# The best expert pairs of a head are sought among 64 sums of sorted key scores in place of 256

## The chip, the cores and the metric

The kernel runs on one core of one Trainium2 chip, as one program. The metric is the device time of one execution in microseconds. Three timed executions of the kernel before are known.

## What is computed

The kernel is one inference step of a trunk of two layers for 544 tokens: 512 of a prompt and 32 of a running stream. Each layer is a mixer (a linear recurrence beside an RWKV-7 state update), then PEER, a retrieval of single-neuron experts, then a small per-layer embedding. The change touches PEER alone. Cut to what matters:

```python
def peer_ffn(xn, wq, keys, u, v):        # per block of 128 tokens
    q = (xb @ wq).reshape(128, 8, 2, 128)                 # 8 heads, 2 query halves each
    s = jnp.einsum('thsc,hskc->thsk', q, keys)            # 128 key scores for each half
    top_s, top_i = lax.top_k(s, 16)                       # sorted, for each half
    cand = top_s[:, :, 0, :, None] + top_s[:, :, 1, None, :]      # 16 x 16 sums
    best_s, best_c = lax.top_k(cand.reshape(128, 8, 256), 16)
    i1 = take_along_axis(top_i[:, :, 0], best_c // 16)
    i2 = take_along_axis(top_i[:, :, 1], best_c % 16)
    e = i1 * 128 + i2                                     # 128 experts for each token
    gate = softmax(best_s)
    hid = einsum('td,tkd->tk', xb, u[e])
    return einsum('tk,tkd->td', gate * gelu(hid), v[e])
```

Both lists of 16 are sorted, falling. So the sum of entry a of the first list and entry b of the second (counted from 0) can be among the 16 best only if (a + 1)(b + 1) is at most 16. That holds for 50 of the 256 pairs.

## The kernel before, in words

**Dense experts.** For 384 of the tokens (three blocks of 128, tile `xh`/`xl`) the kernel computes the inputs of all 16384 experts, in 128 tiles of 128 experts: the PE loop `hidden` (L917 and L920) makes 24 matmuls of 128x384 for each tile (8 parts of the model width, three products of split numbers each). The weights of a tile come by two DMAs of 256 KB from SP (`load_u`), ACT makes the high parts (`high_u`, L1255), the vector engine DVE the low parts (`low_u`, L1887, twice for each tile), PE multiplies, ACT applies gelu (`gelu`, L1262) and stores the result (`save`, L1267, 192 KB). `uh` and `ul` have two buffers each, so ACT may split tile m only when PE has used tile m - 2, and DVE follows ACT.

**Gathered experts.** The other 160 tokens (128 of the prompt, and the 32 of the stream four times, with a quarter of the heads each) take their experts' rows by indirect DMAs from POOL (L620, 512 KB each); DVE takes the dot product of each row (`weigh_row`, L1898).

**Routing.** Which experts a token takes is decided on DVE by `route(part, order, ...)`, in ten parts, once for each block of 128 tokens. For order 1 (the gathered prompt tokens) and orders 3 to 5 (the dense blocks 0 to 2) a block has 16 score lists of 128 keys for 8 heads, for order 2 (the stream) 4 lists for 2 heads. Parts 0 to 4 find the 16 best keys of each list with MAX8 (L1814, L1825), FIND_INDEX8 (L1818, L1829) and MATCH_REPLACE8 (L1819). Part 5 forms all 256 sums of a head (L1834) and takes the first eight maxima (L1838). Part 6 finds their places and strikes them out (L1842, L1843). Part 7 takes the next eight maxima and their places (L1847, L1850). Part 8 subtracts the largest sum (L1855, and releases ACT's exponential), cuts each place into row and column by a shift and a mask (L1856, L1857, L1859) and calls `chosen(0)`, part 9 calls `chosen(1)` and forms gates and expert numbers. `chosen` picks key numbers by comparing each place with 16 numbers, multiplying and summing (L1800, L1803, L1805, 2048 elements each).

**Order of the work.** It is written out by hand. The stage goes over 64 pairs of tiles. Pairs 0 to 4 hold two parts of order 1 each, one behind each tile's `low_u`. Pairs 5 to 7 hold order 2: parts 0 to 3, 4 to 6, 7 to 9. Then there are three dense blocks, each with 10 pairs that hold one part of routing (orders 3 to 5), two `low_u` of two instructions each, and two rows, and 8 pairs that build the gate matrix of the block (`hot`, L1909, and the gate matmuls L954), with four or five rows. At the end stand two pairs with nothing else. During the first 8 pairs of dense blocks 1 and 2, ACT also stores an eighth of the gate matrix of the block before each time (`save_gates`, L1307, 1 MB each, in pieces of 512 bytes); these stores and those of L1267 share ACT's DMA queue, and `gelu` waits until the store of tile m - 2 has landed. After this stage comes one over the 128 tiles of output weights (L993).

**Memory.** All tiles lie at fixed addresses, handed out one behind the other; the table of constants `cn` is among the first, and nearly everything behind it starts where it ends.

Of the kernel before, what the change touches and what calls it, by code (L numbers as in the profile page):

```python
# [9 lines left out]
U32 = mybir.dt.uint32  # L10
# [53 lines left out]
CN = {}  # L64
_at = 0
for _name, _n in [("ident", P), ("ones", P), ("heads", P), ("iota", P), ("causal", P), ("eye", C),
                  ("level", LEVELS * C), ("reset", MW), ("fold", DEC)]:
    CN[_name] = _at
    _at += _n
NCN = _at  # L70

SO = {"conv": (0, 12), "lru": (24, 4), "shift": (32, 14)}
NSO = 60
# [50 lines left out]
def constants():  # L124
    c = np.zeros((P, NCN), np.float32)
    i = np.arange(P)
    c[:, CN["ident"]:CN["ident"] + P] = np.eye(P)
    c[:, CN["ones"]:CN["ones"] + P] = 1.0
    c[:, CN["heads"]:CN["heads"] + P] = (i[:, None] // HD == i[None] // HD)
    c[:, CN["iota"]:CN["iota"] + P] = i[None]  # L130
    s, t = i[:, None] % C, np.arange(C)[None]
    c[:, CN["eye"]:CN["eye"] + C] = s == t
    c[:, CN["causal"]:CN["causal"] + C] = s < t
    c[:, CN["causal"] + C:CN["causal"] + P] = s <= t
    for k in range(LEVELS):
        b = 1 << k
        off = (s // (2 * b) == t // (2 * b)) & (s // b % 2 == 0) & (t // b % 2 == 1)
        c[:, CN["level"] + k * C:CN["level"] + (k + 1) * C] = off
    r = np.ones(MW)
    r[[k * C for k in range(NCH)] + [DEC0]] = 0.0  # L140
    c[:, CN["reset"]:CN["reset"] + MW] = r[None]
    c[:, CN["fold"]:CN["fold"] + DEC] = i[:, None] % DEC == np.arange(DEC)[None]
    return c

# [11 lines left out]
def trunk(nc, x, p, small, const, spread, mixw, wkv0, w_in, w_out, wq, keys, ut, u, v, wple, y, small_out, wkv_out):  # L156
    ctx = ExitStack()
    with ctx:
# [1241 lines left out]
        def _(dve):  # L1400
# [24 lines left out]
            for L in range(DEPTH):  # L1425
# [356 lines left out]

                def route(part, order, n, src, keep):
                    heads = n // 2
                    cand = s2[:, 0:heads * 256].rearrange("p (q a b) -> p q a b", q=heads, a=TOPK)
                    shape = [P, heads, TOPK, TOPK]
                    picks = heads * TOPK
                    eq = s2[:, 0:heads * 256].rearrange("p (q k j) -> p q k j", q=heads, k=TOPK)
# [3 lines left out]
                        return s2[:, q * NK:(q + 1) * NK]  # L1792

                    def pair_of(q):
                        return s2[:, q * 256:(q + 1) * 256]

                    def chosen(w):
                        b3 = bf[:, w, 0:heads, :].rearrange("p q k -> p (q k)").unsqueeze(2).to_broadcast([P, picks, TOPK])
                        i3 = iota[:, 0:TOPK].unsqueeze(1).to_broadcast([P, picks, TOPK])
                        tt(eq3, b3, i3, ALU.is_equal)  # L1800
                        dve.drain()
                        tfs = tf[:, 0:n].rearrange("p (q w) k -> p q w k", w=2)
                        tt(eq, eq, tfs[:, :, w, :].unsqueeze(2).to_broadcast(shape), ALU.mult)  # L1803
                        dve.drain()
                        nc.vector.tensor_reduce(sel_t[:, 1 + w, 0:picks], eq3, AX.X, ALU.add)  # L1805
                        dve.drain()
# [20 lines left out]
                    elif part == 4:  # L1827
                        for q in range(n):
                            mi(ti[:, q, 8:16].bitcast(U32), tv[:, q, 8:16], key(q))  # L1829
                        dve.drain()  # L1830
                    elif part == 5:
                        copy(tf[:, 0:n], ti[:, 0:n].bitcast(U32))
                        tvs = tv[:, 0:n].rearrange("p (q w) k -> p q w k", w=2)
                        tt(cand, tvs[:, :, 0, :].unsqueeze(3).to_broadcast(shape),  # L1834
                           tvs[:, :, 1, :].unsqueeze(2).to_broadcast(shape), ALU.add)
                        dve.drain()
                        for q in range(heads):
                            mx(bv[:, q, 0:8], pair_of(q))  # L1838
                        dve.drain()
                    elif part == 6:  # L1840
                        for q in range(heads):
                            mi(bi[:, q, 0:8].bitcast(U32), bv[:, q, 0:8], pair_of(q))  # L1842
                            mr(pair_of(q), bv[:, q, 0:8], pair_of(q), NEG)  # L1843
                        dve.drain()
                    elif part == 7:
                        for q in range(heads):
                            mx(bv[:, q, 8:16], pair_of(q))  # L1847
                        dve.drain()
                        for q in range(heads):
                            mi(bi[:, q, 8:16].bitcast(U32), bv[:, q, 8:16], pair_of(q))  # L1850
                        dve.drain()
                    elif part == 8:
                        copy(gsum[:, 0:heads], bv[:, 0:heads, 0:1])
                        dve.drain()
                        tt(bv[:, 0:heads], bv[:, 0:heads], gsum[:, 0:heads].unsqueeze(2).to_broadcast([P, heads, TOPK]), ALU.subtract).then_inc(best_ready, 1)  # L1855
                        ts(ba[:, 0, 0:heads].bitcast(U32), bi[:, 0:heads].bitcast(U32), 4, None, ALU.logical_shift_right)  # L1856
                        ts(ba[:, 1, 0:heads].bitcast(U32), bi[:, 0:heads].bitcast(U32), 15, None, ALU.bitwise_and)  # L1857
                        dve.drain()
                        copy(bf[:, :, 0:heads], ba[:, :, 0:heads].bitcast(U32))  # L1859
                        dve.drain()  # L1860
                        chosen(0)
                    else:
                        chosen(1)
                        dve.wait_ge(gexp, L * 5 + order)
                        nc.vector.tensor_reduce(gsum[:, 0:heads], bv[:, 0:heads], AX.X, ALU.add)
                        dve.drain()
                        dve.reciprocal(gsum[:, 0:heads], gsum[:, 0:heads])
                        dve.drain()
                        gate = sel_t[:, 0, :] if keep is None else keep[0]
                        last = tt(gate.rearrange("p (q k) -> p q k", q=heads), bv[:, 0:heads],  # L1870
                                  gsum[:, 0:heads].unsqueeze(2).to_broadcast([P, heads, TOPK]), ALU.mult)
                        if keep is not None:
                            ts(sel_t[:, 1, 0:picks], sel_t[:, 1, 0:picks], float(NK), float(L * NK * NK), ALU.mult, ALU.add)
                            dve.drain()
                            tt(sel_t[:, 1, 0:picks], sel_t[:, 1, 0:picks], sel_t[:, 2, 0:picks], ALU.add)
                            dve.drain()
                            copy(keep[1].bitcast(U32), sel_t[:, 1, 0:picks]).then_inc(rows_ready, 1)
                            dve.drain()
                            dve.sem_inc(routed, 1)
                        else:  # L1880
                            last.then_inc(routed, 1)
# [212 lines left out]
```

## Time and profile before

| | |
|---|---|
| three timed executions | 4023.65, 4023.8, 4024.65 us; median 4023.8 |
| the profiled execution's own time | 4028.22 us |
| its span | 4026.4 us |
| mean granted clock of TensorE, of full speed | 0.959 |
| busy share of the span | PE 90%, DVE 74%, ACT 41%, POOL 23% |
| DMA over the span | 890.04 MB, 221 GB/s |
| instructions | 65006, of them 6048 on DVE |

The page names instructions by engine and line. A line of the page's fifth part gives the busy time of a group of alike instructions, the mean of one, and then the time for which the engine sat idle just before them and what released it. The expert stage of the first layer lies between 608 and 1374 us of the span, that of the second between 2604 and 3371 us.

### The profile page before, as it was taken

To read this page: it belongs to the slowest core of one execution; us is meant where nothing else is said; L and a number is where in the kernel's file an instruction comes from. 1 tells how busy PE (TensorE), PEld (TensorE's weight loads), DVE (VectorE), ACT (ScalarE), POOL (GpSimd) and SP (SyncE) were. 2 spreads that over 40 slices of the span, in tenths; PEclk is the share of its full clock that TensorE was granted. 3 is DMA by queue.
4 is the path that set the end of the run, shared out by engine and by line. 5 is a ranking of instruction groups with operands and counts; after the bars stand their busy time and mean duration, and the time that the engine had idled before them with its cause. 6 is when DMAs were issued, how large, how long until landed. Compare 5 with 4: busy or idle time off the path is not lost.

```text
span 4026.4 us, 65006 instructions
## 1 busy us (share of the span) xinstructions
PE 3629.5 (90%) x24642; PEld 3255.2 (81%) x24642; DVE 2970.4 (74%) x6048; ACT 1654.1 (41%) x3067; POOL 923.9 (23%) x742
## 2 busy tenths in 40 slices
PE   8878897898999799999898878988989897999998
PEld 8867697898988688888787767978989896888877
DVE  5765228989899588888367653199998995888872
ACT  4322123394848433333233221233939393333331
POOL 3200040222223233333031000302323232333320
PEclk9989998999999899999998989999999998999999
DMA  3100135689797999998221001357898989999971
GB/s 118 57 2 3 43 93 182 237 268 344 259 328 270 324 389 381 379 379 312 77 79 47 2 5 53 118 173 246 277 327 275 334 268 340 386 379 380 378 269 62
DMA packets 544661, 890.04 MB, mean 221 GB/s; under 512 B 37824, under 2 KB 361952, under 8 KB 543584
## 3 DMA queue, kind: packets, MB, share of 16 engines
q1 hardware_dynamic: 311872, 444.84, 31.4%
q0 software_dynamic: 92416, 336.17, 23.9%
q10 hardware_dynamic: 140064, 104.88, 8.0%
q8 instruction: 197, 3.23, 0.3%
q14 instruction: 112, 0.92, 0.1%
HBM read 778.07 MB, written 107.67 MB: 220 GB/s over the span
## 4 chain that ended last, share of the span: by engine, by line
PE 67%; DVE 19%; ACT 4%; DMA 3%; issue 3%; ACTq 2%; DVEq 1%; SPq 0%
PE ps L993 26%; PE ps L659 10%; PE ps L643 7%; PE ps L917 6%; PE ps L920 3%; PE ps L954 3%; DVE m L1887 3%; DMA expert_inputs<-m 3%; DVE m L1898 2%; ACT m L1289 2%; PE ps L778 1%; PE ps L786 1%; ACTq L1307 1%; PE ps L635 1%; DVE m L1677 1%
## 5 line engine op out<-in xcount | busy, mean ns | idle before, releaser
L993 PE MATMUL ps<-m,m 128*128 128x512 f32 x4608 | 1066.3, 393 | 12.9 <-DVE m L1959 12.9
L993 PEld LDWEIGHTS ps<-m,m 128*128 128x128 f32 x4608 | 866.8, 188 | 212.2 <-issue 13.5
L917 PE MATMUL ps<-m,m 128*128 128x384 f32 x4096 | 841.7, 348 | 45.3 <-ACT m L1262 45.3
L917 PEld LDWEIGHTS ps<-m,m 128*128 128x128 f32 x4096 | 735.0, 195 | 49.1 <-ACT m L1262 48.6
L620 POOL DMA_INDIRECT m<-in_u,m x320 | 354.0, 1106 | 1092.7 <-DVE m L1898 897.9
L920 PE MATMUL ps<-m,m 128*128 128x384 f32 x2048 | 462.4, 348 | 123.8 <-DVE m L1887 123.7
L620 POOL DMA_INDIRECT m<-in_v,m x320 | 359.7, 1124 | 785.8 <-DVE ps L1971 555.5
L1361 ACT ACTIVATE m<-m 128x1024 fp32r<-128x1024 f32 x256 | 271.5, 1061 | 653.2 <-PE ps L993 651.4
L920 PEld LDWEIGHTS ps<-m,m 128*128 128x128 f32 x2048 | 374.3, 195 | 143.1 <-DVE m L1887 143.0
L659 PE MATMUL ps<-m,m 128*128 128x272 f32 x3648 | 468.7, 290 | 5.4 <-ACT m L1059 4.6
L1255 ACT ACTIVATE m<-m 128x512 fp32r<-128x512 f32 x512 | 318.6, 624 | 374.8 <-PE ps L920 270.7
L659 PEld LDWEIGHTS ps<-m,m 128*128 128x128 f32 x3648 | 463.6, 189 | 8.7 <-issue 5.4
L1887 DVE TENSOR_TENSOR m<-m,m 128x512 fp32r<-128x512 f32 x512 | 331.8, 687 | 83.3 <-ACT m L1255 81.0
L592 POOL TENSOR_TENSOR m<-m,m 128x1024 fp32r<-128x1024 f32 x76 | 191.0, 2515 | 628.1 <-ACT m L1059 628.1
L1971 DVE SCALAR_TENSOR_TENSOR ps<-m,m,ps 128x1024 f32<-128x1024 f32 x254 | 326.0, 1284 | 4.6
L1944 DVE TENSOR_TENSOR m<-m,m 128x1024 fp32r<-128x1024 f32 x256 | 312.0, 1219 | 14.3 <-ACT m L1361 14.3
L1898 DVE CUSTOM_DVE_ANT_0 m<-m,ps 128x1024 f32<-128x1024 f32 x256 | 306.3, 1217 | 6.5 <-issue 0.5
L643 PE MATMUL ps<-m,m 128*128 128x272 f32 x1152 | 274.5, 400 | 39.3 <-DVE m L1756 20.6
L643 PEld LDWEIGHTS ps<-m,m 128*128 128x128 f32 x1152 | 223.3, 194 | 87.4 <-DVE m L1756 21.5
L1909 DVE TENSOR_SCALAR m<-m,m 128x128 f32<-128x128 f32 x768 | 213.0, 347 | 70.5 <-PE ps L954 55.3
L1289 ACT ACTIVATE m<-m,m 128x128 f32<-128x128 f32 x768 | 243.9, 392 | 0.5
L1262 ACT ACTIVATE m<-ps 128x384 f32<-128x384 f32 x256 | 123.8, 484 | 259.1 <-PE ps L920 183.7
(265 smaller groups left out, 3964.7 us busy)
## 6 DMA issues: line engine op xcount, KB each, us to landing
m<-in_ut SPq DMA_DIRECT2D x512, 256.0 KB, 5.3
m<-in_v SPq DMA_DIRECT2D x256, 512.0 KB, 6.2
expert_inputs<-m ACTq DMA_DIRECT2D x256, 192.0 KB, 3.8
gate_matrix<-m ACTq DMA_DIRECT2D x48, 1024.0 KB, 10.2
m<-gate_matrix SPq DMA_DIRECT2D x256, 192.0 KB, 5.2
m<-expert_inputs SPq DMA_DIRECT2D x256, 192.0 KB, 6.8
m<-in_w_in SPq DMA_DIRECT2D x44, 512.0 KB, 3.8
m<-in_wq SPq DMA_DIRECT2D x32, 512.0 KB, 3.8
```

Source lines behind the costliest of these rows:

```text
L620: pool.indirect_dma_start(ug[r % NUG], None, table[:, :], bass.IndirectOffsetOnAxis(ap=index.bitcast(U32), axis=0)).then_inc(row_in[r % NU ...
L643: last = mm(ps[:, bank + a, 0:HALF], wslot[:, slot, k, :], rhs[:, n, a * HALF:(a + 1) * HALF], start=(n == 0), stop=(n == len(ks) - 1))
L659: last = mm(ps[:, 2 * j + a, 0:HALF], lhs[j][:, k, :], rhs[:, k, a * HALF:(a + 1) * HALF], start=(k + w == 0), stop=(k == KD - 1 and w == 2))
L917: mm(ps[:, j, 0:DT], uh[j][:, k, :], x_[:, k, :], start=(k == 0 and x_ is xh), stop=False)
L920: last = mm(ps[:, j, 0:DT], ul[j][:, k, :], xh[:, k, :], start=False, stop=(k == KD - 1))
L993: last = mm(ps[:, 2 * t + a, :], lhs[s][:, t * BLK:(t + 1) * BLK], rhs[s][:, a * 512:(a + 1) * 512], start=(n + w == 0), stop=(n == NK - 1 ...
L1255: av(uh[m % 2][:, ks, :], uraw[m % NU][:, ks, :], ACT.Copy).then_inc(uh_ready, 1)
L1289: av(oneA[:, g % 2, j, :], iota, ACT.Abs, bias=sel[:, 1, t:t + 1])
L1887: tt(ul[m % 2][:, ks, :], uraw[m % NU][:, ks, :], uh[m % 2][:, ks, :].bitcast(F32), ALU.subtract).then_inc(ul_ready, 1)
L1898: nc.vector.tensor_tensor_reduce(row, row, other, 1.0, 0.0, ALU.mult, ALU.add, at).then_inc(row_used, 1)
L1944: tt(vl[n % NV], vraw[n % NV], vh[n % NV].bitcast(F32), ALU.subtract).then_inc(vl_ready, 1)
L1971: last = stt(acc, row, w, acc, ALU.mult, ALU.add)
```

## The change

The 256 sums become 64, in four pieces: row 0 with 16 columns, rows 1 to 3 with 8, rows 4 to 7 with 4, rows 8 to 15 with 1. These hold the 50 pairs. The searches of parts 5 to 7 (L1838, L1842, L1843, L1847, L1850) go over 64 elements for each head. A place in the shorter list is no longer 16 times row plus column: `STARTS` holds the place at which each row begins, in 16 new columns of the constant table. The key number of the row is found in `chosen(0)` as the sum, over all rows that begin at or before the place, of the difference between that row's key number and the one before it. The column is the place masked with 15, 7, 3 or 0, and the mask is worked out by three comparisons with 16, 40 and 56. Part 5 has four additions in place of one, part 8 eight instructions more, so DVE has 11 instructions more for each of the ten orders of the program. Everything else keeps its place in the order. The constant table grows from 1700 to 1716 columns, and the tiles laid out behind it start 64 bytes later.

```diff
+CANDS = [(0, 1, 16), (1, 3, 8), (4, 4, 4), (8, 8, 1)]
+STARTS = [0, 16, 24, 32, 40, 44, 48, 52, *range(56, 64)]
+NCAND = 64
...
-                    cand = s2[:, 0:heads * 256].rearrange("p (q a b) -> p q a b", q=heads, a=TOPK)
+                    cand = s2[:, 0:heads * NCAND].rearrange("p (q c) -> p q c", q=heads)
...
-                        return s2[:, q * 256:(q + 1) * 256]
+                        return s2[:, q * NCAND:(q + 1) * NCAND]
...
-                        i3 = iota[:, 0:TOPK].unsqueeze(1).to_broadcast([P, picks, TOPK])
-                        tt(eq3, b3, i3, ALU.is_equal)
-                        dve.drain()
-                        tfs = tf[:, 0:n].rearrange("p (q w) k -> p q w k", w=2)
-                        tt(eq, eq, tfs[:, :, w, :].unsqueeze(2).to_broadcast(shape), ALU.mult)
+                        i3 = (iota[:, 0:TOPK] if w else const_of("starts", TOPK)).unsqueeze(1).to_broadcast([P, picks, TOPK])
+                        tt(eq3, b3, i3, ALU.is_equal if w else ALU.is_ge)
+                        dve.drain()
+                        tfs = tf[:, 0:n].rearrange("p (q w) k -> p q w k", w=2)[:, :, 1, :] if w else ba[:, 0, 0:heads]
+                        tt(eq, eq, tfs.unsqueeze(2).to_broadcast(shape), ALU.mult)
...
-                        tt(cand, tvs[:, :, 0, :].unsqueeze(3).to_broadcast(shape),
-                           tvs[:, :, 1, :].unsqueeze(2).to_broadcast(shape), ALU.add)
+                        at = 0
+                        for i0, rows_, cols_ in CANDS:
+                            tt(cand[:, :, at:at + rows_ * cols_].rearrange("p q (a b) -> p q a b", a=rows_),
+                               tvs[:, :, 0, i0:i0 + rows_].unsqueeze(3).to_broadcast([P, heads, rows_, cols_]),
+                               tvs[:, :, 1, 0:cols_].unsqueeze(2).to_broadcast([P, heads, rows_, cols_]), ALU.add)
+                            at += rows_ * cols_
...
-                        ts(ba[:, 0, 0:heads].bitcast(U32), bi[:, 0:heads].bitcast(U32), 4, None, ALU.logical_shift_right)
-                        ts(ba[:, 1, 0:heads].bitcast(U32), bi[:, 0:heads].bitcast(U32), 15, None, ALU.bitwise_and)
-                        dve.drain()
-                        copy(bf[:, :, 0:heads], ba[:, :, 0:heads].bitcast(U32))
+                        pos, low = bf[:, 0, 0:heads], ba[:, 1, 0:heads]
+                        firsts = tf[:, 0:n].rearrange("p (q w) k -> p q w k", w=2)[:, :, 0, :]
+                        copy(pos, bi[:, 0:heads].bitcast(U32))
+                        copy(ba[:, 0, 0:heads, 0:1], firsts[:, :, 0:1])
+                        tt(ba[:, 0, 0:heads, 1:TOPK], firsts[:, :, 1:TOPK], firsts[:, :, 0:TOPK - 1], ALU.subtract)
+                        dve.drain()
+                        ts(low, pos, 16.0, -8.0, ALU.is_ge, ALU.mult)
+                        ts(bf[:, 1, 0:heads], pos, 40.0, -4.0, ALU.is_ge, ALU.mult)
+                        dve.drain()
+                        stt(low, low, 15.0, bf[:, 1, 0:heads], ALU.add, ALU.add)
+                        dve.drain()
+                        ts(bf[:, 1, 0:heads], pos, 56.0, -3.0, ALU.is_ge, ALU.mult)
+                        dve.drain()
+                        tt(low, low, bf[:, 1, 0:heads], ALU.add)
+                        dve.drain()
+                        copy(bf[:, 1, 0:heads].bitcast(U32), low)
+                        dve.drain()
+                        tt(low.bitcast(U32), bf[:, 1, 0:heads].bitcast(U32), bi[:, 0:heads].bitcast(U32), ALU.bitwise_and)
+                        dve.drain()
+                        copy(bf[:, 1, 0:heads], low.bitcast(U32))
                         dve.drain()
                         chosen(0)
```

## Rows read from the trace of the kernel before

**Rows 1.** The page, part five: PE's second group of the dense experts.
```profile
L920 PE MATMUL ps<-m,m 128*128 128x384 f32 x2048 | 462.4, 348 | 123.8 <-DVE m L1887 123.7
```

**Rows 2.** Windows: length, each engine's busy us (xinstructions), PE clock, DMA share, GB/s.
```profile
635.00:692.10 57.10, 41.39 (x194) 39.45 (x193) 54.45 (x168) 16.03 (x27) 5.21 (x5) 0.85 0.38 130
723.10:758.70 35.60, 34.20 (x194) 33.16 (x193) 34.78 (x144) 13.18 (x25) 9.16 (x8) 1.00 0.83 281
758.70:791.20 32.50, 28.31 (x146) 27.67 (x145) 31.94 (x92) 9.84 (x18) 6.87 (x6) 0.89 0.67 231
791.20:816.70 25.50, 19.90 (x98) 19.23 (x97) 24.57 (x29) 9.34 (x15) 4.52 (x4) 0.87 0.56 194
928.30:966.00 37.70, 34.83 (x196) 33.63 (x196) 32.76 (x129) 12.71 (x24) 9.16 (x8) 1.00 1.07 368
966.00:998.60 32.60, 26.94 (x144) 25.98 (x143) 32.11 (x92) 9.80 (x20) 6.87 (x6) 0.95 1.06 357
998.60:1026.00 27.40, 20.23 (x99) 19.55 (x98) 24.77 (x30) 9.37 (x16) 4.59 (x5) 0.88 0.73 244
...
3134.50:3171.40 36.90, 34.38 (x195) 33.42 (x194) 32.71 (x129) 12.63 (x24) 9.16 (x8) 1.00 1.06 359
...
1500.00:1900.00 400.00, 400.00 (x1736) 325.43 (x1735) 354.53 (x410) 141.50 (x193) 134.04 (x119) 1.00 1.00 375
```

**Rows 3.** DVE's timeline, parts 5 to 8 of dense block 1, first layer: start, length.
```profile
966.17 0.29 DVE L1832 CAST m<-m 128x256 f32<-128x256 uint32 x1
966.38 2.29 DVE L1834 TENSOR_TENSOR m<-m 128x2048 f32<-128x2048 f32 x1
968.73 2.72 DVE L1838 MAX8 m<-m 128x8 f32<-128x256 f32 x8
971.57 1.22 DVE L1898 CUSTOM_DVE_ANT_0 m<-m,ps 128x1024 f32<-128x1024 f32 x1
...
976.26 0.09 DVE L1842 MATCH_VALUE_LOAD m<-m,m 128x8 f32 x1
...
982.77 1.22 DVE L1898 CUSTOM_DVE_ANT_0 m<-m,ps 128x1024 f32<-128x1024 f32 x1
...
987.47 2.70 DVE L1847 MAX8 m<-m 128x8 f32<-128x256 f32 x8
...
993.62 1.22 DVE L1898 CUSTOM_DVE_ANT_0 m<-m,ps 128x1024 f32<-128x1024 f32 x1
...
998.32 0.29 DVE L1853 COPY m<-m 128x8 f32<-128x8 f32 x1
998.68 0.29 DVE L1855 TENSOR_TENSOR m<-m,m 128x128 f32<-128x128 f32 x1
998.89 0.22 DVE L1856 TENSOR_SCALAR m<-m 128x128 uint32<-128x128 uint32 x1
...
999.69 2.29 DVE L1800 TENSOR_TENSOR m<-m,m 128x2048 f32<-128x2048 f32 x1
```

**Rows 4.** DVE's timeline: the same searches over 128 elements, dense block 2.
```profile
1135.40 0.08 DVE L1818 MATCH_VALUE_LOAD m<-m,m 128x8 f32 x1
...
1135.92 0.08 DVE L1818 MATCH_VALUE_LOAD m<-m,m 128x8 f32 x1
...
1155.06 3.18 DVE L1825 MAX8 m<-m 128x8 f32<-128x128 f32 x16
```

**Rows 5.** DVE's timeline: small instructions of which each needs the one before.
```profile
680.86 0.22 DVE L1873 TENSOR_SCALAR m<-m 128x128 f32<-128x128 f32 x1
681.16 0.29 DVE L1875 TENSOR_TENSOR m<-m 128x128 f32<-128x128 f32 x1
681.52 0.23 DVE L1877 CAST m<-m 128x128 uint32<-128x128 f32 x1
```

**Rows 6.** ACT's timeline, gelu of every tile: an undisturbed pair of tiles.
```profile
928.31 0.49 ACT L1262 ACTIVATE m<-ps 128x384 f32<-128x384 f32 x1 [1.39 <-PE ps L920]
...
936.63 0.49 ACT L1262 ACTIVATE m<-ps 128x384 f32<-128x384 f32 x1 [0.86 <-PE ps L920]
```

**Rows 7.** Waits from 930 to 1000 us: total, times, longest.
```profile
ACT m L1262 <- DMA expert_inputs<-m: 16.1, 4, 6.0
```

**Rows 8.** DMA queues from 928 to 975 us: ACT's queue, packets, MB, share.
```profile
q10 hardware_dynamic: 11073, 6.85, 45.9%
```

More of the change, by code:

```diff
@@ L66 @@
 for _name, _n in [("ident", P), ("ones", P), ("heads", P), ("iota", P), ("causal", P), ("eye", C),
-                  ("level", LEVELS * C), ("reset", MW), ("fold", DEC)]:
+                  ("level", LEVELS * C), ("reset", MW), ("fold", DEC), ("starts", TOPK)]:
     CN[_name] = _at
@@ L141, in constants @@
     c[:, CN["reset"]:CN["reset"] + MW] = r[None]
+    c[:, CN["starts"]:CN["starts"] + TOPK] = np.array(STARTS)[None]
     c[:, CN["fold"]:CN["fold"] + DEC] = i[:, None] % DEC == np.arange(DEC)[None]
```

## The prediction

> **What bounds the kernel now.** The change touches only routing on DVE, so I first asked where DVE sets the pace. The page's fifth part gives the answer for the dense experts: PE idled 123.8 us before its last product, nearly all for `low_u` on DVE [rows 1]. The window view says in which pairs. One undisturbed pair of tiles takes 8.32 us from gelu to gelu, which is PE alone [rows 6]. In parts 1 to 4 of dense block 0 a pair takes 35.60 / 4 = 8.9 us. In parts 5 to 7 it takes 32.50 / 3 = 10.8 us, with DVE busy for 31.94 and PE for 28.31. Parts 8 and 9 take 25.50, of which DVE works 24.57 [rows 2]. There DVE is the bound, and the searches over 256 sums are exactly its parts 5 to 7. The same holds for order 1 (635.0 to 692.1: DVE 54.45 of 57.10, PE 41.39) [rows 2].
>
> Dense blocks 1 and 2 differ. Parts 1 to 4 need no more DVE time than in block 0, yet take 37.70 us (36.90 in the fastest of four such windows), with a DMA share of 1.06 or 1.07 [rows 2], and ACT's gelu waits for its stores to land, 16.1 us in 70 [rows 7]. ACT's queue, where the gate matrix goes out in 512-byte pieces, takes 45.9% of the DMA engines' time [rows 8]. In parts 5 to 7 (32.60 us) the DMA share is still 1.06 [rows 2], so DVE and the DMA engines are both full. This second bound is what the sum must respect.
>
> **DVE time of one order with 8 heads.**
> Part 5 now runs from 966.17 to 971.57, 5.40 us [rows 3]. Eight MAX8 over 256 take 2.72 us, one every 0.33 us; sixteen over 128 take 3.18 us, one every 0.19 [rows 3, 4]. That is 1.06 ns for each element, so one over 64 should come every 0.126 us: 1.6 us less. The sums shrink from 2048 elements to 512, 1.6 us less at 1.04 ns each, with three more instructions at some 0.07 (estimate): 1.4 less. Part 5 saves 3.0 and lasts 2.4.
> Part 6 runs from 976.26 to 982.77, 0.80 us a head after its closing gap [rows 3]. A head's two searches over 128 take 0.52 [rows 4], so over 64 they take 0.38. It saves 3.3 and lasts 3.2.
> Part 7 (987.47 to 993.62, 6.15 us [rows 3]) saves 1.6 on MAX8 and half of part 6's on FIND_INDEX8, 1.7. It saves 3.3 and lasts 2.9.
> Part 8 grows. Its small work takes 1.37 us now (998.32 to 999.69) [rows 3]. The new chain is 13 instructions, mostly each needing the last. Such a step costs 0.30 us behind a scalar instruction and 0.36 behind others [rows 5], one that needs nothing 0.1 to 0.2 (0.21 at 998.68 [rows 3]). I get 0.36 + 0.21 + 0.2 + 0.36 + 0.43 + 0.36 + 0.30 + 4 x 0.36 = 3.7 us, so 2.3 more. ACT's exponential is released before this chain and is no later. `chosen` does the same three instructions of 2048 elements.
> Together: 9.6 less, 2.3 more, 7.3 us of DVE time less.
>
> **What of it reaches the end.**
> *Dense block 0, twice (one in each layer).* Parts 5 to 7 would need 32.5 - 9.6 = 22.9 us of DVE, but PE needs 3 x 8.4 = 25.2. So these pairs save 7.3, and DVE gains up to 2.3 us on PE. It can use this lead in part 8, as far as the two buffers let it run ahead; I take 1.7 of the 2.3. Parts 8 and 9 get 0.6 longer. Sum: 2 x -6.7 = -13.4 (bounds -5.5 and -7.2 each).
> *Dense blocks 1 and 2, four times.* Here the DMA pace is late next. Parts 1 to 4 ran at it: 36.9 to 38.0 us for four pairs, 9.35 on the mean of my four windows (two of them stand in [rows 2]). At that pace three pairs take 28.1 us, a saving of 4.5 (from 32.6), and 3.9 with the 0.6. Sum: 4 x -3.9 = -15.6. The bounds are the PE floor, -7.2 each, and -1.5 each, if the queue of stores, which the slow pairs let run down, now grows instead.
> *Order 1, twice.* No rows and no gate stores are moved there (DMA share 0.38 [rows 2]). Three tiles need 3 x 1.2 + 2.4 + 3.2 + 2.9 = 12.1 of DVE against 12.5 of PE, so nearly all 7.3 show: 2 x -7.1 = -14.2 (bounds -6 and -7.4).
> *Order 2, twice, with 2 heads.* At these rates its searches save 2 us and part 8's chain of short instructions adds about 1.7, but the saving falls mostly into the pair of parts 4 to 6, where PE is the bound, and the addition into the pair of parts 7 to 9, where DVE is: 2 x +0.5 = +1.0 (bounds -0.5 and +1 each).
> *At nothing:* 64 bytes more of constants for each partition at the start, behind 2 MB of inputs; the first gather starts 7 us earlier, but its rows are due at fixed pairs; the second half of each block (`hot`) and the output stage are PE's.
>
> Sum: -13.4 - 15.6 - 14.2 + 1.0 = -42.2 us. The profiled execution took 4028.2, so its like should take 3986.0. The median of the timed runs is 4.4 below the profiled one, so I predict 3981.6.
>
> **One rule that speaks against the change.** All tiles behind the constants move by 64 bytes. The gate matrix before its stores lies at byte 16512 + 4 x 36680, which is 160 past a multiple of 256, and will lie at 224 past. No row here shows the price of an offset; the stores already start off such a boundary and take 45.9% of the DMA time [rows 8]. I take nothing for it in the sum.
> The Trainium skill, DMA: Bandwidth & Descriptors, section "How a descriptor splits into AXI transactions", says that a read that does not start at a multiple of 256 bytes is fetched from the multiple below, and the unused bytes cost as well. By it a piece of 512 bytes would fetch 736 bytes in place of 672, some 10% more. No run so far shows whether that matters.
>
> **The rivals.**
> *B, the DMA keeps up.* If pairs at PE's pace are possible in blocks 1 and 2, each of the four gives -6.8 in place of -3.9: 3970.0. For it speaks that the pairs moved 357 GB/s in parts 5 to 7 and 368 in parts 1 to 4, so there is some room; against it the share of 1.06 in both [rows 2]. Chance 0.12.
> *C, the DMA gives less than before.* If the pieces of ACT's queue take 10% longer, its 45.9% [rows 8] make the saturated pairs 4.6% slower: 9.35 to 9.78 us, for 7 pairs in each of four blocks, +12: 3993.6. A queue that never drains would look alike. Chance 0.13. (The rule above is one way to this.)
> *D, short searches don't get shorter.* Below 128 elements the fixed part may rule. If 64 elements cost what 128 cost, 40 searches give back 0.07 us each, 2.7 us of DVE for an order: all of it in order 1 (+5.4), the lead and 0.4 in block 0 (+4.2), nothing where DMA is the bound: 3991.2. For it: nothing shorter than 128 is in the trace. Against it: the step from 256 to 128 is as large as the elements explain [rows 3, 4]. Chance 0.11.
> *E, slower.* The moved addresses cost where the DMA engines are full for long: in the output stage, DMA share 1.00, 375 GB/s, PE busy 400 of 400 us [rows 2]. That stage has 4608 matmuls, 1736 in 400 us, so 1062 us. From 4.0% on (42.2 / 1062) it eats the gain; at 6% it gives +64, 4045.6. Against it: nothing changes there but 64 bytes of offset. Chance 0.02.
> That the change doesn't do what it says I rule out: 110 more instructions stand in DVE's program, 11 for each of ten orders, as they should.
> TensorE's clock was at 1.2 GHz for a while in the DVE-bound windows (mean 0.89, 0.87, 0.95, 0.88, against 1.00 in the others) [rows 2], each time where PE had been waiting. While DVE is the bound such a dip is free. With PE busy it should not come in parts 5 to 7; if it came, it would cost up to 3.6 us in a window (11% of 32.5). That is inside the range.
>
> **How the numbers follow.** Forecast 0.60, B 0.12, C 0.13, D 0.11, E 0.02, and 0.02 for a gain lost in ways I don't see. A difference under 0.2% (8 us) is about what a measurement of this kernel can't tell from no change. With all the good bounds at once the gain is 59 (3965), with all the bad ones 26 (3998); these ends hold B, C and D. Faster 0.96, same 0.02, slower 0.02.
>
> **What would show it.** MAX8 at L1838's place every 0.13 us, and part 6 near 3.2 us. Parts 5 to 7 of block 0 in about 25 us, with PE full and its clock at 1.00; in blocks 1 and 2 in about 28, with more waits of gelu for its stores. Part 8's small work 3.7 us. Parts 8 and 9 nearly as long as before. If blocks 1 and 2 save as much as block 0, B is right; if their parts 1 to 4 get longer too, C; if the searches show 0.19, D. The output stage must stay at 4.15 us a tile.

## The result, and the profile after

| | median of the timed executions | lowest to highest |
|---|---|---|
| before, 4 executions | 4023.73 us | 4023.33 to 4024.65 |
| changed kernel, 4 executions | 3993.24 us | 3987.98 to 3995.32 |

The ratio is 0.9916, with a 95% interval of 0.9903 to 0.9928. So the change saves 30.5 us of the 42.2 forecast. A second comparison (e2 below) gave 0.9909 (0.9894 to 0.9924), 36.9 us. The profiled execution has a span of 3989.4 us against 4026.4, 37.0 less. So a single execution or a single comparison moves by several us here, which is part of what follows. One execution of the kernel before, beside e5 to e8, took 5509.13 us at a granted clock of 0.608 and is left out of every comparison below.

The page of the changed kernel answers to [rows 1] with its line L925. The chain of waits that ended last stands above it.

```profile
PE 68%; DVE 16%; DMA 5%; ACT 5%; issue 3%; ACTq 2%; DVEq 1%; SPq 0%
...
L925 PE MATMUL ps<-m,m 128*128 128x384 f32 x2048 | 457.8, 346 | 90.3 <-DVE m L1912 90.0
```

PE's wait for `low_u` fell from 123.8 to 90.3 us. In the chain, the transfers rose from 3% to 5% and DVE fell from 19% to 16%.

**The searches themselves.** Parts 5 to 8 on DVE's timeline in dense block 0 (start, length), which answer to [rows 3]:

```profile
748.42 0.41 DVE L1837 CAST m<-m 128x256 f32<-128x256 uint32 x1
748.75 0.88 DVE L1841 TENSOR_TENSOR m<-m 128x128 f32<-128x128 f32 x4
749.70 1.11 DVE L1847 MAX8 m<-m 128x8 f32<-128x64 f32 x8
750.93 1.22 DVE L1923 CUSTOM_DVE_ANT_0 m<-m,ps 128x1024 f32<-128x1024 f32 x1
...
755.63 0.09 DVE L1851 MATCH_VALUE_LOAD m<-m,m 128x8 f32 x1
...
758.95 1.22 DVE L1923 CUSTOM_DVE_ANT_0 m<-m,ps 128x1024 f32<-128x1024 f32 x1
...
763.64 1.11 DVE L1856 MAX8 m<-m 128x8 f32<-128x64 f32 x8
...
766.60 1.22 DVE L1923 CUSTOM_DVE_ANT_0 m<-m,ps 128x1024 f32<-128x1024 f32 x1
...
771.30 0.29 DVE L1862 COPY m<-m 128x8 f32<-128x8 f32 x1
...
774.88 2.29 DVE L1805 TENSOR_TENSOR m<-m,m 128x2048 f32<-128x2048 f32 x1
```

Part 5 takes 2.51 us (748.42 to 750.93), forecast 2.4. Part 6 takes 3.32 (755.63 to 758.95), forecast 3.2. Part 7 takes 2.96 (763.64 to 766.60), forecast 2.9. Part 8's small work takes 3.58 (771.30 to 774.88), forecast 3.7. Together DVE saves 18.06 - 8.79 = 9.3 us and pays 2.2, so 7.1 for an order; the forecast was 7.3.

**Where it reached the end.** Windows of the changed kernel, with the columns of [rows 2]. In order: order 1 (with the first pair of order 2); block 0 parts 1 to 4, 5 to 7, 8 and 9; block 1 the same three; block 2 the same three; the output stage.

```profile
632.40:682.70 50.30, 38.94 (x194) 37.98 (x193) 46.84 (x183) 16.07 (x28) 5.22 (x5) 0.83 0.44 147
713.50:748.70 35.20, 34.11 (x194) 33.15 (x193) 34.74 (x144) 13.14 (x25) 9.17 (x8) 1.00 0.83 281
748.70:773.70 25.00, 25.00 (x146) 25.00 (x145) 24.13 (x103) 9.92 (x19) 6.91 (x7) 1.00 0.96 319
773.70:801.20 27.50, 20.31 (x99) 19.58 (x98) 24.78 (x29) 9.32 (x16) 4.59 (x4) 0.88 0.53 190
912.70:950.60 37.90, 34.80 (x196) 33.62 (x196) 32.96 (x129) 12.75 (x24) 9.29 (x8) 1.00 1.07 368
950.60:981.50 30.90, 29.23 (x164) 27.96 (x163) 25.01 (x106) 9.44 (x19) 6.89 (x6) 1.00 1.07 390
981.50:1006.90 25.40, 15.96 (x79) 14.97 (x77) 24.41 (x27) 9.39 (x17) 4.59 (x4) 0.87 0.67 222
1118.40:1154.90 36.50, 34.27 (x193) 33.17 (x193) 33.00 (x130) 12.81 (x24) 9.15 (x8) 1.00 1.07 366
1154.90:1189.00 34.10, 27.80 (x146) 27.48 (x146) 24.43 (x104) 9.63 (x19) 7.02 (x7) 0.90 1.01 342
1189.00:1214.80 25.80, 19.31 (x98) 18.63 (x97) 24.66 (x29) 9.32 (x15) 4.58 (x4) 0.87 0.64 218
...
1500.00:1900.00 400.00, 399.76 (x1753) 325.59 (x1751) 346.98 (x400) 139.93 (x189) 127.92 (x113) 1.00 0.95 358
```

In block 0 parts 5 to 7 went from 32.50 to 25.00 us, with PE busy for all of it and its clock at 1.00. In block 1 they took 30.90 and in block 2 even 34.10, against 32.60 and 32.5 before, though DVE's work fell from about 32 to 25.01 and 24.43. The DMA share is over 1.00 there in both. The waits of the changed kernel from 950 to 982 us (total, times, longest) say what holds them:

```profile
ACT m L1267 <- DMA expert_inputs<-m: 12.9, 3, 5.1
...
ACT m L1260 <- issue: 3.0, 1, 3.0
...
ACT m L1260 <- DMA m<-in_ut: 2.7, 2, 1.4
```

That is gelu waiting for its own stores. Over the whole execution these waits came to 95.7 us in 24, against 75.0 in 20 before. In block 2 one of them lasted 8.19 us. It stands in ACT's timeline (start, length, engine; the idle time before it in brackets):

```profile
1163.79 4.07 ACTq L1272 DMA_DIRECT2D expert_inputs<-m  x1
1167.90 0.46 ACTq L1312 DMA_DIRECT2D gate_matrix<-m  x1
1168.47 0.64 ACT L1260 ACTIVATE m<-m 128x512 fp32r<-128x512 f32 x1 [4.19 <-issue]
1177.30 0.49 ACT L1267 ACTIVATE m<-ps 128x384 f32<-128x384 f32 x1 [8.19 <-DMA expert_inputs<-m]
```

Put together by the sections of the stage (each counted from the start of one gelu to that of a later one, order 1 from the first `low_u` of the stage; both layers added, one profile each):

| section | before | changed | difference | forecast |
|---|---|---|---|---|
| order 1, pairs 0 to 4 | 139.4 | 125.6 | -13.8 | -14.2 |
| order 2, pairs 5 to 7 | 69.5 | 68.6 | -0.9 | +1.0 |
| block 0, parts 1 to 9 | 187.0 | 175.2 | -11.8 | -13.4 |
| blocks 1 and 2, parts 1 to 9, four in all | 387.7 | 378.2 | -9.6 | -15.6 |
| everything else | | | -0.9 | 0 |
| span | 4026.4 | 3989.4 | -37.0 | -42.2 |

### The profile page after: what moved, and what is told of

The parts are those of the page before. It is cut to its first block, busy times and chain, and to the rows that moved or that the text cites. A ratio compares the mean times of both kernels' runs of the same rounds, so it can differ in the third digit from the quotient of the medians.

```text
span 3989.4 us, 65176 instructions
## 1 busy us (share of the span) xinstructions
PE 3621.7 (91%) x24642; PEld 3248.9 (81%) x24642; DVE 2908.6 (73%) x6158; ACT 1652.7 (41%) x3067; POOL 925.1 (23%) x742
## 3 DMA queue, kind: packets, MB, share of 16 engines
q1 hardware_dynamic: 311872, 444.85, 31.6%
q10 hardware_dynamic: 140064, 104.88, 8.1%
## 4 chain that ended last, share of the span: by engine, by line
PE 68%; DVE 16%; DMA 5%; ACT 5%; issue 3%; ACTq 2%; DVEq 1%; SPq 0%
PE ps L998 27%; PE ps L664 11%; PE ps L648 7%; PE ps L922 7%; DMA expert_inputs<-m 5%; PE ps L925 4%; PE ps L959 3%; DVE m L1912 2%; ACT m L1294 2%; DVE m L1923 2%; PE ps L783 1%; PE ps L791 1%; ACTq L1312 1%; PE ps L640 1%; DVE m L1682 1%
## 5 line engine op out<-in xcount | busy, mean ns | idle before, releaser
L998 PE MATMUL ps<-m,m 128*128 128x512 f32 x4608 | 1067.8, 394 | 11.5 <-DVE m L1984 11.5
L925 PE MATMUL ps<-m,m 128*128 128x384 f32 x2048 | 457.8, 346 | 90.3 <-DVE m L1912 90.0
L925 PEld LDWEIGHTS ps<-m,m 128*128 128x128 f32 x2048 | 373.3, 194 | 104.1 <-DVE m L1912 104.1
L648 PE MATMUL ps<-m,m 128*128 128x272 f32 x1152 | 275.1, 401 | 38.6 <-DVE m L1761 20.6
## 6 DMA issues: line engine op xcount, KB each, us to landing
gate_matrix<-m ACTq DMA_DIRECT2D x48, 1024.0 KB, 12.8
```

The source lines that it names most:

```text
L648: last = mm(ps[:, bank + a, 0:HALF], wslot[:, slot, k, :], rhs[:, n, a * HALF:(a + 1) * HALF], start=(n == 0), stop=(n == len(ks) - 1))
L925: last = mm(ps[:, j, 0:DT], ul[j][:, k, :], xh[:, k, :], start=False, stop=(k == KD - 1))
L998: last = mm(ps[:, 2 * t + a, :], lhs[s][:, t * BLK:(t + 1) * BLK], rhs[s][:, a * 512:(a + 1) * 512], start=(n + w == 0), stop=(n == NK - 1 ...
```

## The experiments

Two theories stood against each other for the missing part. DMA-BOUND: what DVE frees in blocks 1 and 2 goes to the DMA engines, which move the gate stores, the weights, the rows and the small stores there at their limit. ADDRESSES: the 64 bytes by which everything moved make the stores dearer.

**e1 to e4, one chip.** e1 and e3 add spare columns to the constants, to the kernel before and to the changed one:

```diff
-                  ("level", LEVELS * C), ("reset", MW), ("fold", DEC)]:
+                  ("level", LEVELS * C), ("reset", MW), ("fold", DEC), ("spare", 16)]:
...
-                  ("level", LEVELS * C), ("reset", MW), ("fold", DEC), ("starts", TOPK)]:
+                  ("level", LEVELS * C), ("reset", MW), ("fold", DEC), ("starts", TOPK), ("spare", 48)]:
```

> The kernel before with 16 spare columns behind its constants, so that all tiles behind them start 64 bytes later, as in the change, and nothing else differs. Theory DMA-BOUND (in blocks 1 and 2 the time freed on DVE goes to the DMA engines, whatever the addresses): within 2 us of the kernel before, parts 5 to 7 of those blocks 32.5 us as before. Theory ADDRESSES (the offset makes ACT's stores about 10% dearer): parts 1 to 4 of blocks 1 and 2 get longer than 37.4 us by 1 to 2 us each, the whole 4 to 12 us slower. The Trainium skill, DMA: Bandwidth & Descriptors, section How a descriptor splits into AXI transactions, would have the pieces at 224 bytes past a multiple of 256 fetch 736 bytes in place of 672.

> The changed kernel as it is, again. Both theories: 3988 to 3996 us. DMA-BOUND: the sections of block 0 and of order 1 are the same as in the first profile to 0.5 us, and the spread between executions lies in blocks 1 and 2, parts 1 to 9 (first profile: 94.1, 96.4, 93.5, 94.2 us). If the spread lies elsewhere, the theory is wrong about it.

> The changed kernel with 48 more spare columns, so that the tiles behind the constants lie 256 bytes later than before the change and at the same place within a multiple of 256 as then. DMA-BOUND: as e2, within 3 us. ADDRESSES: faster than e2 by 4 to 12 us, all of it in blocks 1 and 2.

Measured: e1 4029.59 us against 4026.69 for the kernel before, a ratio of 1.0005 (0.9996 to 1.0014). e2 3989.77 us, ratio 0.9909 (0.9894 to 0.9924). e3 3994.72 us, 0.9916 (0.9902 to 0.9929). Moving all tiles by 64 bytes costs nothing that shows, and moving them back to the old place within 256 bytes gains nothing. The interval leaves room for 0.14%, 5.6 us, and e1's median is 2.9 us up, a little more than the 2 expected of DMA-BOUND. But parts 1 to 4 of blocks 1 and 2, which ADDRESSES had to make 1 to 2 us longer each, add up to 150.2 us in e1 against 149.7, and the packets of ACT's queue took the same share of the DMA engines' time. Its line on the page of the kernel before, and on that of e1 (packets, MB, share):

```profile
q10 hardware_dynamic: 140064, 104.88, 8.0%
```
```profile
q10 hardware_dynamic: 140064, 104.88, 8.0%
```

ADDRESSES falls, and with it the part of rival C that rested on it.

The sections of e1 to e3 also answer the question of the spread. Parts 5 to 7 of block 0 are 25.0 us in every profile of the changed kernel. Parts 1 to 9 of blocks 1 and 2 add up to 387.7 us in the first profile of the kernel before and 380.6 in e1; to 378.2 in the first profile of the changed kernel, 373.6 in e2 and 376.4 in e3. So the same program differs there by 5 to 7 us from one execution to the next. e2 expected that the spread would lie there alone; it does not quite, since order 1 of e3's first layer took 66.5 us instead of 62.8, and of e1 72.4 instead of 69.6. That excess stands before the first gelu, where PE waited 3.11 and 2.18 us for nothing that the profile shows; from the first gelu on, the order took as long as in the first profiles.

e4 moves rows away from the pairs that the DMA engines bound:

```diff
-                n += 2 if b is None or i < ROUTE_PAIRS else 4
+                if b is None or i < ROUTE_PAIRS:
+                    n += 1 if b and 0 < i < 8 else 2
+                else:
+                    n += 5 if b < NB - 1 and i > ROUTE_PAIRS else 4
```

> The changed kernel with one gathered row in place of two in pairs 1 to 7 of dense blocks 1 and 2, and five in place of four in pairs 11 to 17 of blocks 0 and 1. This takes 0.5 MB of 3.5 from each DMA-bound pair. DMA-BOUND: parts 1 to 7 of blocks 1 and 2 fall from about 69 us to PE's floor of 58 to 60 each, 9 us each, four times; pairs 11 to 17 stay at 12.6 us if DVE (11.3 + 1.2 = 12.5 us) still fits; the whole 30 to 38 us faster than e2, near 3958. If DVE doesn't fit there, 28 pairs get 0.2 to 0.5 us longer and the gain is 20 to 30. ADDRESSES: the stores stay dear, but the bytes fall as well, so it gives a smaller gain of 10 to 20 us.

Measured: 3964.96 us, ratio 0.9845 (0.9832 to 0.9859), 24.8 us faster than e2 and less than the 30 to 38 expected. Windows of e4: four gate pairs of block 0, then parts 1 to 4, 5 to 7, 8 and 9 of block 2.

```profile
833.30:883.80 50.50, 50.33 (x333) 49.39 (x333) 49.91 (x124) 49.40 (x122) 19.20 (x20) 1.00 0.93 323
1116.10:1149.50 33.40, 33.40 (x195) 33.29 (x194) 29.75 (x130) 12.88 (x25) 4.57 (x4) 1.00 1.05 368
1149.50:1174.40 24.90, 24.90 (x145) 24.90 (x144) 20.12 (x94) 9.75 (x18) 3.24 (x4) 1.00 1.08 371
1174.40:1201.20 26.80, 19.12 (x99) 18.45 (x98) 25.47 (x31) 9.35 (x15) 4.55 (x4) 0.87 0.63 216
```

Parts 1 to 7 now run at PE's floor in block 2, with the DMA engines just able to follow (368 and 371 GB/s, at a share of 1.05 and 1.08, as high as where PE had to wait), and the gate pairs hold five rows with DVE busy for 49.91 of 50.50 us and no loss. In block 1 parts 1 to 4 still took 36.5 and 35.8. Another part of the expected gain was lost again in parts 8 and 9: 27.8, 26.8, 28.5 and 26.3 us in place of 25.4, 28.0, 26.5 and 24.2 in e2. The likely reason is that while gelu waits for the DMA, PE and DVE work ahead of it, and these windows are bounded by gelu; such work is done before part 8's window opens. The first profile shows it: 164 matmuls of PE in parts 5 to 7 of block 1 where block 0 has 146, and 79 in parts 8 and 9 where block 0 has 99. A stall of this kind is paid back in part, and only the sum over parts 1 to 9 can be read.

**e5 and e6, the stores out of the way.** In both kernels the gate matrix is stored only at the end of the stage, and ACT's waits for these stores move with it (left out here). What is stored is then the matrix of the last block three times, so the results are wrong and only the times of the sections are of use:

```diff
-                    if b is not None and b > 0 and i < 8:
-                        save_gates(b - 1, i)
-                    elif pair == PART - 1:
-                        for q in range(8):
-                            save_gates(NB - 1, q)
+                    if pair == PART - 1:
+                        for to in range(NB):
+                            for q in range(8):
+                                save_gates(to, q)
```

> The changed kernel in which the gate matrix of blocks 0 and 1 is not stored during blocks 1 and 2: the staging tile is stored three times at the end of the stage instead (so all blocks get the gates of the last, and the last pairs of the stage get longer by some 40 us). Read by sections only. DMA-BOUND: parts 5 to 7 of blocks 1 and 2 take 25.0 us as in block 0, parts 1 to 4 35 to 35.5 or less. If something else than the stores holds these pairs back, they stay at 28 us or more.

> The same edit on the kernel before. DMA-BOUND: parts 1 to 4 of blocks 1 and 2 fall from 37.4 to about 35.4 us, parts 5 to 7 stay at 32.3 to 32.5 (DVE is the bound there), so that e5 against e6 gives about 5.5 us for each of six dense blocks, 47 us with order 1. If the stores were no bound in parts 1 to 4, those stay at 37.

Measured, one execution each. Windows of e5, block 1, parts 1 to 4, 5 to 7, 8 and 9:

```profile
917.30:950.70 33.40, 33.40 (x194) 33.26 (x194) 32.94 (x130) 13.19 (x25) 9.15 (x8) 1.00 0.93 313
950.70:975.70 25.00, 25.00 (x146) 25.00 (x145) 24.05 (x102) 9.92 (x19) 6.89 (x7) 1.00 0.94 324
975.70:1003.30 27.60, 20.16 (x98) 19.43 (x97) 24.95 (x30) 9.34 (x16) 4.58 (x4) 0.88 0.53 189
```

Windows of e6, block 1, parts 1 to 4, 5 to 7:

```profile
928.90:962.20 33.30, 33.30 (x193) 33.16 (x192) 32.84 (x130) 13.13 (x24) 9.10 (x8) 1.00 0.95 318
962.20:994.50 32.30, 27.43 (x147) 26.47 (x146) 31.81 (x91) 9.88 (x18) 6.92 (x7) 0.95 0.69 234
```

Without the stores all four blocks behave like block 0, in parts 5 to 7 of both layers: 25.0 in e5, 32.2 to 32.5 in e6. Gelu waits for no store any more in either. Between the two kernels the spans differ by 4128.4 - 4072.4 = 56.0 us, and parts 1 to 9 of blocks 1 and 2 by 367.5 - 339.8 = 27.7 us. That is the 27 us that rival B gave these blocks (4 x 6.8). So the searches are worth 56 us where the DMA has room, the kernel gets 37 in its profile, and the stores of the gate matrix in the same pairs take nearly all of the difference. This settles that it is these stores; whether by their bytes or by their place in ACT's queue is left to e11. I had expected less: 5.5 us for each dense block and 47 in all, where block 0 gave 6.0, blocks 1 and 2 6.9 each, and the whole 56, and parts 1 to 4 at 35.4 us, where PE's floor was 33.4. The last two pairs got longer by some 60 us each layer and not by 40, in both kernels alike.

**e7, the price of the chain in part 8.** The short searches stay, the cutting of places is the old one:

```diff
-                        copy(pos, bi[:, 0:heads].bitcast(U32))
...
+                        ts(ba[:, 0, 0:heads].bitcast(U32), bi[:, 0:heads].bitcast(U32), 4, None, ALU.logical_shift_right)
+                        ts(ba[:, 1, 0:heads].bitcast(U32), bi[:, 0:heads].bitcast(U32), 15, None, ALU.bitwise_and)
+                        dve.drain()
+                        copy(bf[:, :, 0:heads], ba[:, :, 0:heads].bitcast(U32))
```

> The changed kernel with the kernel before's cutting of places (shift and mask, and the comparison with equal), so that the eight added instructions of part 8 are gone and the short searches stay; experts are then the wrong ones. Prediction's account: part 8's small work falls from 3.7 to 1.4 us, parts 8 and 9 get shorter by 2.3 us in each of six dense blocks and in order 1 twice, 1.7 in order 2 twice: up to 22 us faster than the changed kernel, if nothing else catches it. RIVAL: lead of DVE over PE hides the chain, less than 8 us.

Measured: 3970.21 us, ratio 0.9862 (0.9846 to 0.9878), 19.6 us faster than e2 by the medians and 18.9 by the two ratios. Parts 8 and 9 of block 0 fall from 27.5 to 25.6 and from 27.2 to 25.3 us, order 1 from 63.1 to 60.1 and from 62.7 to 60.3. In blocks 1 and 2 parts 1 to 9 went from 373.6 to 366.4 us together, 1.8 for each block. The rival, that DVE's lead hides the chain, falls. I had let the lead hide 1.7 of 2.3 us in each block. In truth 1.9 of 2.2 show. Why the lead hides so little was not tried. e7 picks other experts and so gathers other rows; that this costs or saves nothing is not shown.

**e8, the rows moved in the kernel before.** The edit of e4.

> The rows moved as in e4, on the kernel before. DMA-BOUND: parts 1 to 4 gain the DMA's 2 us and DVE's row, parts 5 to 7 are DVE's there and lose one row of 1.2 us each: 32.5 to 29; together 5 to 7 us for each of the four blocks, 20 to 28 us. Then e4 minus this is what the short searches give with room on the DMA side, 40 us or more. RIVAL (the gain of e4 comes from the rows alone): e8 gains as much as e4 did, and the searches add no more than the 37 us of e2.

Measured: 4000.70 us against 4026.3, ratio 0.9936 (0.9922 to 0.995), 25.6 us. Parts 5 to 7 of blocks 1 and 2 took 28.7, 28.7, 28.7 and 28.3 us, as expected. The moved rows gain about the same in either kernel (24.8 and 25.6), and the searches are worth 36.1 us with the rows moved (61.7 - 25.6) as against 36.9 without. These are the rival's numbers, and the first expectation (40 or more) missed. e8 alone would speak against DMA-BOUND; the sections say why it does not: moving rows frees not only the DMA engines but also 1.14 us of DVE in each of these pairs, and what the searches could still save there down to PE's 25.0 us is then only 3.6 in place of 7.3, and parts 8 and 9 of e4 give back 1.2 us of that in each block (109.4 us for the four against 104.6 in e8).

**e9 and e10, better versions.** e9 is e4 with no rows in pairs 8 and 9 of blocks 1 and 2 and five in the gate pairs of block 2; e10 takes them out of block 0 as well:

```diff
+                if b is None:
+                    n += 2
+                elif i < ROUTE_PAIRS:
+                    n += 0 if i > 7 else 1 if b and i > 0 else 2
+                else:
+                    n += 5
```

> As e4, and besides no rows at all in pairs 8 and 9 of dense blocks 1 and 2, where DVE is the bound (part 8 with its longer chain, part 9); these eight rows of a layer go to the last eight gate pairs, of block 2, five in place of four. Each row taken away there frees 1.14 us of DVE: parts 8 and 9 of those blocks fall from 27 to about 22.5 us, four times, the gate pairs of block 2 stay at 101 us. The whole 14 to 18 us faster than e4, near 3948. RIVAL: PE or the short lead takes over in parts 8 and 9 and less than 8 us show.

> As e9, and no rows in pairs 8 and 9 of block 0 either; of these four rows of a layer two go to the first gate pairs of blocks 0 and 1 (five rows each) and two to pair 62, where DVE is idle for 29 of 32 us. Parts 8 and 9 of block 0 fall from 27.5 to 23 us, twice; the first gate pairs, 14.8 us with DVE 13.1 busy, get up to 1 us longer each. The whole 5 to 9 us faster than e9. RIVAL: the two rows in pair 62 lengthen that pair, where the DMA engines are full, by 1 to 3 us each layer, and the gain is 2 to 5.

Measured: e9 3950.98 us, ratio 0.9813 (0.98 to 0.9827), 14.0 faster than e4 by the medians, 12.9 by the ratios, at the low end of the 14 to 18 expected. Parts 8 and 9 of blocks 1 and 2 took 23.9, 23.3, 24.1 and 22.7 us, most of them above the 22.5 expected. e10 3947.52 us, 0.9807 (0.9794 to 0.982), 3.5 faster than e9 by the medians, with intervals that overlap, so the 5 to 9 expected did not come and whether e10 is faster than e9 is open. In e10 parts 8 and 9 of block 0 went to 22.5 us (27.5 in e9's first layer). Pairs 62 and 63 together, of which pair 62 got two rows, went from 40.8 us in the first layer and 41.2 in the second to 42.6 and 42.5, which is the rival's price. Windows of e10, parts 8 and 9 of blocks 0 and 1:

```profile
773.20:795.70 22.50, 18.83 (x98) 18.15 (x98) 20.29 (x21) 9.35 (x15) 0.00 (x0) 0.92 0.46 157
968.50:992.10 23.60, 18.49 (x98) 17.81 (x97) 21.07 (x24) 9.31 (x15) 0.00 (x0) 0.93 0.61 207
```

e10 has the lowest median of this study: 78.7 us under the kernel before on its chip (4026.21).

**e11 and e12, queue or bytes.** Gelu waits for small stores that stand behind a big one in the same queue, so the order in the queue could be what costs, and not the bytes. Both versions store the gate matrix from SP's queue, one pair later, in the changed kernel and in e10:

```diff
+                    if b and 0 < i < 9 and m % 2 == 0:
+                        q = i - 1
+                        sp_.wait_ge(gmat_out, (L * NB + b) * GB)
+                        sp_.dma_start(gate_d[:, 16 * q:16 * q + 16, (b - 1) * BLK:b * BLK], stage[:, 16 * q:16 * q + 16, :]).then_inc(gate_saved[q // 2], 16)
...
-                    if b is not None and b > 0 and i < 8:
-                        save_gates(b - 1, i)
-                    elif pair == PART - 1:
+                    if pair == PART - 1:
```

> The changed kernel with the gate matrix of blocks 0 and 1 stored from SP's queue, one eighth at a time one pair later (pairs 1 to 8 of the next block), so that ACT's small stores no longer stand behind a store of 1 MB and ACT no longer issues into a full queue. The bytes are the same. BYTES (the DMA engines' throughput is the bound, about 350 to 375 GB/s): parts 1 to 9 of blocks 1 and 2 stay at 91 to 96 us each and the whole within 5 us of e2. QUEUE (gelu waits for its store behind the big one in the same queue, and that is what holds PE back): those parts fall to 88 us or less and the whole is 10 to 25 us faster than e2; gelu's waits for DMA go away.

> The same on the fastest version, e10, where the rows are moved as well. Parts 1 to 4 of block 1, 36 us there against PE's 33.4, are what is left of the DMA bound. BYTES: within 3 us of e10. QUEUE: parts 1 to 4 of block 1 fall to 33.5 and the whole is 3 to 6 us faster.

Measured: e11 3995.45 us, ratio 0.9922 (0.9908 to 0.9936), 5.7 slower than e2 by the medians. e12 3960.51 us, 0.9829 (0.9814 to 0.9844), 13.0 slower than e10 by the medians and 8.9 by the ratios; parts 1 to 4 of block 1 took 38.6 and 36.5 us there and did not fall. Waits of e11 from 907 to 990 us:

```profile
ACT m L1264 <- DMA m<-in_ut: 53.8, 17, 6.8
DVE m L1914 <- ACT m L1264: 11.9, 12, 2.9
```

Gelu no longer waits for its stores, and instead ACT waits 53.8 us for the weights, which stand behind the big store in SP's queue. Parts 1 to 9 of blocks 1 and 2 add up to 373.4 us in e11 and 373.6 in e2, so over these parts the order in the queue does not decide. But part 0 grew from 8.7 to 12.9, 9.5, 12.4 and 9.2 us; the stall moved to the weights and began earlier. The theory BYTES holds for the sum over the parts. It missed e11 by a little (5 us at most expected) and e12 clearly (3 at most): the growth of part 0, in e12 to 13.0, 16.1, 12.7 and 12.8 us, is what it left out. Larger pieces than 512 bytes were not tried, so the number of pieces is not told apart from their bytes.

## Why the prediction was right or wrong

The measured 3993.24 us lies 11.6 above the 3981.6 forecast and inside the range of 3965 to 3998. (The bad bounds add up to 27 and not 26, which would make the range end at 3997.) Faster was right.

*DVE's time for the parts* was right: 9.3 us less and 2.2 more for an order, forecast 9.6 and 2.3. Rival D, whose 3991.2 us is also close to the measured time, falls with that: a MAX8 over 64 comes every 0.13 us.

*Order 1* was right (-13.8 against -14.2). *Order 2* came out on the other side of zero by 1 us each layer (-0.9 in all against +1.0): the pair of parts 4 to 6 stayed at PE's 8.32 us, and the pair of parts 7 to 9 got no longer (11.5 and 12.2 us before, 11.3 and 11.0 after). That DVE's lead from the one pair hid the chain in the other is the likely reading, but was not tried.

*Block 0, parts 5 to 7*, was right to 0.1 us: 25.0 against 25.2. The step that failed there is the lead. "I take 1.7 of the 2.3" was too much: parts 8 and 9 grew by 2.0 and 1.4 us and not by 0.6, and e7 gives 1.9 for the chain. That is 2 us of the sum. (In e1, with the old searches, these parts took 27.4 us in one layer, where the first profile of the kernel before has 25.5; so e7's number is the better one.)

*Blocks 1 and 2* are the mis-sized term: -15.6 forecast, -9.6 in the first profile, and -8.1 between the mean of two profiles of the old code (387.7 and e1's 380.6) and the mean of three of the new (378.2, 373.6, 376.4). The mechanism was named and is shown by e5 and e6. By the same means, for one block, parts 1 to 4 went from 37.5 to 37.7 us, parts 5 to 7 from 32.1 to 30.6 where 28.1 was forecast, and parts 8 and 9 from 26.4 to 25.8. The size failed at "9.35 on the mean of my four windows": each of those windows begins with a pair at 8.3 us, before gelu has to wait for a store [rows 6]. The other three pairs took 37.7 - 8.3 = 29.4, so 9.8 each, and that was the pace to take for pairs that start with a full queue. At 9.8 parts 5 to 7 come to 29.4; measured were 30.9, 34.0, 31.3 and 31.5 in the first profile and 27.8, 28.6, 29.5 and 32.9 in e2. The bytes say the same. In [rows 2] parts 5 to 7 moved 357 GB/s for 32.60 us, 11.6 MB. At the 368 GB/s of parts 1 to 4 these take 31.6 us; in 28.1 us they would need 414 GB/s, and no window shown here went over 390. The other error has the other sign: parts 8 and 9 did not grow by 0.6 us. In the first two profiles they even fell from 27.4, 27.4, 27.3 and 25.9 to 25.4, 25.8, 25.0 and 25.6, but e1 has 25.9, 25.9, 25.9 and 25.9 with the old searches, so by the means it is 0.6 us less. That is still less than the 2.2 us of the chain would give, and fits PE's work ahead while gelu waits.

*Rival B* was wrong here and right about its condition: e5 against e6 gives these blocks the 27 us. *Rival C*, at 3993.6, has the measured time to 0.4 us, and that is luck: its 10% on the pieces was not there, and parts 1 to 4 did not get longer as it said they would. It was right only in that a queue that does not drain would look alike. e1, with the stores at 224 bytes past a multiple of 256, has a ratio of 1.0005 (0.9996 to 1.0014), and e3, with them back at 160, is not faster than e2. The rule of the Trainium skill that the prediction weighed (DMA: Bandwidth & Descriptors, "How a descriptor splits into AXI transactions") says that bytes in front of such a start are fetched though unused, and cost as well. They may well be fetched, but in this kernel the stores' time does not follow them. *Rival E* falls by the same runs, and the output stage kept its pace: 1753 matmuls recorded in 400 us against 1736 [rows 2].

*The clock* did as forecast: 1.00 in parts 5 to 7 of block 0, where it was 0.89. In block 2 of the first layer it fell to 0.90 in those parts, where gelu waited 8.19 us for a store and PE was busy for 27.80 of 34.10 us.

## What to carry to other kernels

When an engine is freed, read first what the other resource does in the same pairs. A DMA share at or over 1.00 there is a warning that the time may go to the transfers, however exactly the instructions were costed. It is no proof, since e4 ran at PE's floor with 1.05 and 1.08; so work out how many GB/s the forecast time would need. Take a queue's pace from pairs that begin with a full queue, and read a stalled stretch together with what follows it, since work done ahead pays back part of a stall. And once the bound has moved, move the work: 26 rows of each layer (14 in e4, 8 more in e9, 4 more in e10), shifted to pairs with room, gave as much again as the change itself (e2 to e10, 42 us by the medians and 41 by the ratios).

## What the runs showed of the hardware

- On DVE, MAX8, FIND_INDEX8 and MATCH_REPLACE8 keep their slope down to 64 elements: the mean of one was 213, 220 and 210 ns over 64 against 277, 285 and 275 over 128 and 412, 420 and 409 over 256, and neighbours overlap by some 80 ns, so a MAX8 over 64 comes every 0.13 us.
- A DMA that ACT issues behind large stores in its own queue can hold ACT's instructions: in blocks 1 and 2 of the first layer one issue of 192 KB took 4.07 us where 0.33 is the median, and the next split of weights waited 4.19 us for it. Without the 1 MB stores in that queue (e5, e6, e11) no such issue there took over 0.36 us.
- Where a store of 512-byte pieces begins within 256 bytes of SBUF, at 160 or at 224, shows in no time: 8.0% of the DMA engines' time for ACT's 140064 packets in either case.
- A mix of 512-byte pieces, weights and gathered rows ran at 342 to 390 GB/s with a DMA share of 1.01 to 1.08. That is no worse than the output stage's 358 to 375.
- The same program differs by up to 10 us between executions on one chip (before: 4020.9 to 4031.1 in 15). In the profiles the sections that differ most are those where the DMA engines are full, by 5 to 7 us of some 380.
